# Last feed-forward of a two-block transformer: the down projection set three pairs of tiles behind the gate and up products, in place of two

## What is computed

```
def conv_ffn(h, w_up, taps, conv_b, w_down, rows):
    a, g = jnp.split(h @ w_up, 2, axis=-1)          # width 2816 each
    gc = lax.conv_general_dilated(g2, tp[:, :, None, :].astype(g.dtype), (1, 1), 'SAME', ...)
    gc = gc.reshape(bsz, t, f) + conv_b
    return (a * jax.nn.gelu(gc, approximate=False)) @ w_down

        x = x + g2 * conv_ffn(h2, w_up[l], conv_w[l], conv_b[l], w_down[l], rows)
    return rmsnorm(x, norm_final)
```

## Time and profile before

| what | value |
|---|---|
| median of three executions | 1308.42 us |
| the profiled execution: its time | 1310.74 us |
| its span, first to last instruction | 1308.9 us |
| mean granted TensorE clock | 0.975 |
| TensorE busy over the span | 1220.5 us, 93% |
| VectorE busy | 964.2 us, 74% |
| ScalarE busy | 601.6 us, 46% |
| GpSimd busy | 217.9 us, 17% |

### The profile page before, as it was taken

How to read it: one execution, slowest core, us unless ns; L and a number is a source line. 1 busy time by engine, 2 the same in 40 slices (tenths; PEclk the granted TensorE clock), 3 DMA queues, 4 the chain that set the end, 5 groups by cost and what they waited for, 6 DMA issues and landing times.

```text
span 1308.9 us, 21913 instructions
## 1 busy us (share of the span) xinstructions
PE 1220.5 (93%) x9222; PEld 1133.2 (87%) x9222; DVE 964.2 (74%) x1338; ACT 601.6 (46%) x818; POOL 217.9 (17%) x138
## 2 busy tenths in 40 slices
PE   3999989899999999999899999999899988999997
PEld 3888878677899999996577999999799887999996
DVE  6767665655479886565875699785659946999996
ACT  4464243233554444646365675444442444455442
POOL 0000000000244543000000132222000003344441
PEclk9999899899999999999999999999899998999999
DMA  8351001000577765553322779885352333545540
GB/s 279 132 173 65 2 33 66 1 1 1 193 265 251 255 227 180 169 168 120 105 97 97 255 279 322 287 287 180 110 181 97 101 110 112 181 160 181 188 161 33
DMA packets 122080, 199.74 MB, mean 153 GB/s; under 512 B 3200, under 2 KB 110080, under 8 KB 111744
## 3 DMA queue, kind: packets, MB, share of 16 engines
q1 hardware_dynamic: 117088, 168.11, 38.0%
q0 software_dynamic: 3456, 25.17, 5.4%
q10 hardware_dynamic: 1440, 5.08, 1.1%
HBM read 197.30 MB, written 1.05 MB: 152 GB/s over the span
## 4 chain that ended last, share of the span: by engine, by line
PE 63%; DVE 26%; ACT 6%; issue 4%; DMA 0%; DVEq 0%; ACTq 0%
PE bank L661 11%; PE bank L663 11%; PE bank L662 11%; DVE ring_r L1848 8%; DVE buf L2587 6%; PE bank L748 4%; PE bank L749 4%; PE bank L750 4%; ACT high L1261 4%; DVE work L2139 2%; PE bank L947 2%; DVE work L2135 2%; PE bank L935 2%; PE bank L677 1%; PE bank L1149 1%
## 5 line engine op out<-in xcount | busy, mean ns | idle before, releaser
L661 PE MATMUL bank<-part,high 128*128 128x256 f32 x1664 | 474.1, 285 | 29.0 <-DVE part L1855 22.5
L663 PE MATMUL bank<-part,ring_r 128*128 128x256 f32 x1664 | 468.3, 281 | 0.0
L662 PE MATMUL bank<-part,high 128*128 128x256 f32 x1664 | 468.3, 281 | 0.0
L1848 DVE TENSOR_TENSOR ring_r<-ring,high 128x2048 fp32r<-128x2048 f32 (+1 forms) x155 | 343.3, 2222 | 117.5 <-ACT high L1261 116.7
L1261 ACT ACTIVATE high<-ring 128x2048 fp32r<-128x2048 f32 x155 | 295.6, 1910 | 188.0 <-PE bank L663 135.3
L661 PEld LDWEIGHTS bank<-part,high 128*128 128x128 f32 x1664 | 316.3, 190 | 35.1 <-issue 17.5
L662 PEld LDWEIGHTS bank<-part,high 128*128 128x128 f32 x1664 | 316.1, 190 | 1.3 <-issue 1.2
L663 PEld LDWEIGHTS bank<-part,ring_r 128*128 128x128 f32 x1664 | 316.3, 190 | 0.0
L1776 POOL TENSOR_TENSOR ring_r<-ring,high 128x512 fp32r<-128x512 f32 x44 | 87.9, 2000 | 483.7 <-ACT high L1261 483.7
L748 PE MATMUL bank<-part,high 128*128 128x256 f32 x528 | 150.4, 285 | 5.7 <-DVE ring_r L1848 5.7
L1770 POOL TENSOR_TENSOR part<-buf,part 128x256 fp32r<-128x256 f32 x65 | 116.7, 1797 | 225.9 <-ACT part L1327 225.9
(11 more groups left out here) (276 smaller groups left out, 1555.5 us busy)
## 6 DMA issues: line engine op xcount, KB each, us to landing
ring<-in_wide SPq DMA_DIRECT2D x122, 1024.0 KB, 5.9
ring<-in_down SPq DMA_DIRECT2D x33, 1024.0 KB, 4.9
buf<-in_wide POOLq DMA_DIRECT2D x24, 1024.0 KB, 5.9
con<-in_cons SPq DMA_DIRECT2D x1, 1536.0 KB, 11.1
ring<-in_wide SPq DMA_DIRECT2D x2, 576.0 KB, 7.0
buf<-in_wide ACTq DMA_DIRECT2D x1, 1024.0 KB, 5.2
buf<-in_wide SPq DMA_DIRECT2D x1, 1024.0 KB, 5.3
buf<-in_ctx_t ACTq DMA_DIRECT2D x1, 1024.0 KB, 6.6
```

The lines of the kernel that those rows point to most:

```text
L661: mm(bank, ah, bh, start=start, stop=False, skip_group_check=shared)
L662: mm(bank, ah, bl, start=False, stop=False, skip_group_check=shared)
L663: return mm(bank, al, bh, start=False, stop=stop, skip_group_check=shared)
L1848: v.tensor_tensor(low, raw, hi.bitcast(F32), ALU.subtract).then_inc(sem("unit_low"), 1)
```

## The change

The one constant `LAG = 2` becomes `LAGS = (2, 2, 3)`, indexed by the feed-forward. For the first two the order stays as it was. For the last, the stream, the bank plan, TensorE's order and the `ahead` calls of ScalarE and VectorE all use 3, so TensorE goes g0 g1 g2 g3 d0 g4 d1 ... g10 d7, and d8, d9, d10 are left for the list behind the loop. On VectorE the last turn's `ahead` for a down unit moves from the end of the loop to behind the low part of tile 21; ScalarE's already stood behind `gate_high` of tile 21.

```diff
-LAG = 2
+LAGS = (2, 2, 3)
...
     def ffn(n):
         for c in range(PAIR_N):
             out.extend((f"gu{n}", c, half, "wide", W_AT[f"gu{n}"][0] + c) for half in range(2))
-            if c >= LAG:
-                out.append((f"dn{n}", c - LAG, 0, "down", PAIR_N * n + c - LAG))
-        out.extend((f"dn{n}", c, 0, "down", PAIR_N * n + c) for c in range(PAIR_N - LAG, PAIR_N))
+            if c >= LAGS[n]:
+                out.append((f"dn{n}", c - LAGS[n], 0, "down", PAIR_N * n + c - LAGS[n]))
+        out.extend((f"dn{n}", c, 0, "down", PAIR_N * n + c) for c in range(PAIR_N - LAGS[n], PAIR_N))
...
-                        if c >= LAG:
-                            down_pair(n, c - LAG)
-                    w = [arrived(f"dn{n}", c, 0) for c in range(PAIR_N - LAG, PAIR_N)]
-                    rest = range(FT - 2 * LAG, FT)
+                        if c >= LAGS[n]:
+                            down_pair(n, c - LAGS[n])
+                    w = [arrived(f"dn{n}", c, 0) for c in range(PAIR_N - LAGS[n], PAIR_N)]
+                    rest = range(FT - 2 * LAGS[n], FT)
...
-                    if f % 2 and LAG <= f // 2 < PAIR_N - 1:
-                        ahead("dn2", f // 2 - LAG, 0)
+                    if f % 2 and LAGS[2] <= f // 2 < PAIR_N - 1:
+                        ahead("dn2", f // 2 - LAGS[2], 0)
                 gate_high(2, FT - 2)
                 gelu_of(FT - 1)
                 gate_high(2, FT - 1)
-                ahead("dn2", PAIR_N - 1 - LAG, 0)
+                ahead("dn2", PAIR_N - 1 - LAGS[2], 0)
                 down(2, 7)
...
-                    if f % 2 and f // 2 >= LAG:
-                        ahead("dn2", f // 2 - LAG, 0)
+                    if f % 2 and LAGS[2] <= f // 2 < PAIR_N - 1:
+                        ahead("dn2", f // 2 - LAGS[2], 0)
                 gated(2, FT - 1, slice(0, S))
                 eng.wait_ge(sem("act_high"), 3 * FT)
                 eng.wait_ge(sem("act_ready"), 3 * FT - 1)
                 v.tensor_tensor(act_low(FT - 1), act_value(FT - 1), act_high(FT - 1).bitcast(F32), ALU.subtract).then_inc(sem("act_ready"), 1)
+                ahead("dn2", PAIR_N - 1 - LAGS[2], 0)
                 down_resid(2, lambda cb, bank: v.scalar_tensor_tensor(resid[:, cb, :], bank, ada[:, 40 + cb, 0:1], resid[:, cb, :],
```

More of the change, by code:

```diff
@@ L257, in plan_ffn @@
                     place(key, FFN_BANKS)
-                if c == LAG:
+                if c == LAGS[n]:
                     for j in range(KT // 2):
                         place_at(("dn", n, j), j)
-                if c >= LAG:
-                    unit_mid(f"dn{n}", c - LAG, 0)
+                if c >= LAGS[n]:
+                    unit_mid(f"dn{n}", c - LAGS[n], 0)
             for key in after_first:
                 place(key, FFN_BANKS)
-            for c in range(PAIR_N - LAG, PAIR_N):
+            for c in range(PAIR_N - LAGS[n], PAIR_N):
                 unit_job(f"dn{n}", c, 0, ("dn", n, KT // 2 - 1))
@@ L784, in feed_forward @@
                                 pe.wait_ge(sem("act_ready"), FT * n + f + 1)
-                            last = down_tile(n, f, cb, w[f // 2 - PAIR_N + LAG])
+                            last = down_tile(n, f, cb, w[f // 2 - PAIR_N + LAGS[n]])
                         if cb % 2:
@@ L1345, in ffn @@
                             between(f // 2)
-                            if f // 2 >= LAG:
-                                ahead(f"dn{n}", f // 2 - LAG, 0)
+                            if f // 2 >= LAGS[n]:
+                                ahead(f"dn{n}", f // 2 - LAGS[n], 0)
                 def down(n, norm_no):
@@ L1939, in ffn @@
                         between(f)
-                        if f % 2 and f // 2 >= LAG:
-                            ahead(f"dn{n}", f // 2 - LAG, 0)
+                        if f % 2 and f // 2 >= LAGS[n]:
+                            ahead(f"dn{n}", f // 2 - LAGS[n], 0)
                 for ap, value in ((one_col, 1.0), (eps_lnx, LNX_EPS), (eps_sub, SUBLN_EPS)):
```

## The result

| | before | after |
|---|---|---|
| median of four executions each | 1308.42 us | 1322.87 us |
| the profiled execution: its time | 1310.74 us | 1323.33 us |
| its span | 1308.9 us | 1321.5 us |
| first gate/up matmul to the start of the last down matmul | 199.99 us | 213.37 us |

The change made the kernel slower: the ratio is 1.0088, with a 95% interval from 1.0056 to 1.0121, that is 7.3 to 15.8 us. The forecast was 1322.6. It leaves out what the earlier stages do differently from one execution to the next; in the profiled one after, the stage began 0.8 us earlier.

The account below looks back on a forecast made before the run. TensorE and VectorE were both taken as full, VectorE setting the pace. The last matmul, at 1294.1 + 16.85 + 1.8 = 1312.75 against 1298.54, comes 14.2 us later: 1308.4 + 14.2 = 1322.6 us, range 1317 to 1328.

Parts of the forecast that it names:

- (a): Front of the last feed-forward: TensorE waits for banks 1.7 us before tile 6 and 2.0 before tile 7, at no cost.
- (b): From tile 6 on: VectorE has one down unit fewer behind it and leads by 2.2 us at tile 21's taps.
- (c): Tail: d10's split falls behind tile 21's low part; the list holds d8, d9 and d10, TensorE idle some 14 us.
- (d): Last 144 matmuls to the end: 16.85 us plus 1.8 for the clock's restart (1.6 to 3.5); last matmul 14.2 us later.
- Rival 1: VectorE, middle pairs: it escapes its collisions with GpSimd, so only +5.6 us, 1314.0 us, no change; 4%.
- Rival 2: Tail: the list does not hold d8 and d9, each waits only for itself; +2.7 us, 1311.1 us, no change; 4%.
- Rival 3: Front: the 3.7 us of bank waits reach VectorE and the lead is lost; slower still, 1325 to 1328.5 us; 11%.
- Rival 4: Where TensorE waits for activations: the longer lag helps and the kernel gets faster; the two waits total 5.1 us; 1%.

Follow-up runs that it names:

- e1: The changed kernel with the list of waits ahead of the last down matmuls taken out; ratio 1.0027, stage 201.14 us.
- e3: The changed kernel without the list of waits and with d10 split ahead of tile 21's taps; ratio 1.0000, stage 199.06 us.
- e5: The kernel before (lag 2) with the list of waits taken out; ratio 0.9966, stage 196.78 us.
- e2: The changed kernel, list kept, with rounding and split of d10 moved back ahead of tile 21's taps; ratio 1.0058, stage 206.09 us.
- e4: The changed kernel with the list cut to d9 and d10, so d8 runs straight behind d7; ratio 1.0063, median 1317.86 us.

## Why the prediction was right

**(a) The first pairs.** Expected: 1.7 us before tile 6, 2.0 before tile 7, free of cost in the changed kernel. TensorE waited 1.67 and 1.68 us at 1130.48 (tile 5) and 1138.05 (tile 6), 0.64 at 1144.58 (tile 7). So tile 6 came as expected, while the wait before tile 5 was not foreseen and the one before tile 7 was far shorter than said. VectorE's rows of the taps of tiles 2 and 4 in the kernel after show both misses, and the first two rows here, of TensorE and VectorE in the kernel before, what they stand against (tile 4's taps took 5.66 us there):

```profile
1130.49 0.35 PE L661 MATMUL bank<-part,high 128*128 128x256 f32 x1 [0.63 <-DVE buf L1918]
```
```profile
1125.40 4.61 DVE L2587 SCALAR_TENSOR_TENSOR buf<-buf,col 128x256 f32<-128x256 f32 x8
```
```profile
1124.36 5.65 DVE L2587 SCALAR_TENSOR_TENSOR buf<-buf,col 128x256 f32<-128x256 f32 x8
...
1139.49 4.61 DVE L2587 SCALAR_TENSOR_TENSOR buf<-buf,col 128x256 f32<-128x256 f32 x8
```

Tile 2's taps took 1.0 us more and tile 4's 1.0 less than before, and so in every kernel here with a lag of three; the prediction had kept both as they were. The waits before tiles 5, 6 and 7 came to 4.0 us, where the forecast had 3.7 before tiles 6 and 7 and left out what the kernel before already waits before tile 5, 0.63: that the sums are near each other is luck, since the two misses cancel. In the changed kernel the waits were free, as VectorE reached tile 21 ahead of the kernel before all the same (b), and e1, with all of them, is only 1.2 us behind it in the stage. e3 against e5 shows their price where the tail hides nothing. e3's bank waits are 3.3 us longer (4.69 against 1.35, the 0.72 before tile 4 in both), e5 waits 1.4 us in the tail that e3 doesn't, and the stages lie 2.3 apart; so the front costs about 3.7 us there, restarts of the clock included.

**(b) The middle.** Expected: VectorE 2.2 us ahead by tile 21's taps. From the stage's start they began at 1282.32 - 1097.72 = 184.60, before at 187.38: 2.8 ahead, of which 2.3 is d10's split itself; the other half microsecond is no more than readings of one program differ by.

**(c) The tail.** This was the step that counted. Expected start of the last 144 matmuls 195.55 us into the stage, after 14 us of idle; measured 195.03 after 13.97. e1 and e2 show the two causes apart: without the list the idle is 1.90 us, with the split in its old place it is 5.62, with neither there is none (e3).

**(d) The clock.** Expected 1.8 us for the restart, at most 3.5. The last 143 spacings took 18.34 us where 0.1178 each give 16.85: 1.5 us, a little under my lower bound of 1.6. The windows of the kernel after:

```profile
1278.80:1292.70 13.90, 0.00 (x0) 0.00 (x0) 11.11 (x16) 5.08 (x7) 2.98 (x2) 0.62 0.00 0
1292.70:1296.70 4.00, 3.95 (x21) 3.98 (x22) 0.00 (x0) 0.00 (x0) 0.00 (x0) 0.60 0.00 0
1296.70:1300.70 4.00, 4.00 (x36) 4.00 (x35) 0.00 (x0) 0.00 (x0) 0.00 (x0) 1.00 0.01 4
```

The granted clock (the third number from the end) had fallen during the idle time, was 0.60 in the first 4 us of work and full from there. The sum, 0.5 us too late at the start of the run and 0.3 too much for the clock, gives 14.2 against the 13.4 of the stage. The medians lie 14.45 us apart, the spans 12.6, and the interval of the ratio reaches from 7.3 to 15.8 us, so that forecast and median agree to 0.3 us is luck; what the runs bear out is the hold and its size.

**The rivals.** Rival 1 did not come: VectorE's 176 taps took 107.0 us in all, before 106.8 for the same number, so it lost as much to collisions as ever, though single tiles lost more or less than before (a). Rival 2 was priced at +2.7 us for a kernel in which the list does not hold d8 and d9; e1 is that kernel and came to +1.2 in the stage, the difference being the restart that a wait of 1.90 us did not cost. Rival 3, the front, is right as a mechanism and wrong for this kernel: it costs only where nothing hides it. Its premise that a slow restart follows each wait over 2 us does not hold in the changed kernel, as the last section shows. Rival 4, a gain by later activations, had nothing to gain from.

## What to carry to other kernels

A longer lag helps only against waits for what it delays: look at what ends the idle stretches (here splits of weights and banks, not activations) before lengthening it. Whatever lies behind the loop grows with the lag, so the tail has to be read as a chain of its own: which unit's buffer comes free by what, where in each engine's order its preparation is written, and whether a wait for the last unit stands ahead of work that is ready. Waits written just where they are needed are worth more here than the lag: taking the list out of the kernel before won 3.2 us of the stage by the removal of one line.

## What was not expected of the hardware

The restart of TensorE's clock cost about the same whatever the idle stretch before it. Against 0.1178 us a matmul the runs behind the last hold took 1.5 us more after 13.97 us of idle, 1.8 after 8.67 (e4: 12.95 us for 95 spacings), and 2.0 after 5.62 (e2: 1302.05 - 1283.25 = 18.80 us for 143). After 1.90 us, in e1, it was 0.1. My upper bound, which let the cost grow with the idle time, was not needed.

Whether a wait of some 2 us is followed by a slow restart can't be read from its length. The 6 us behind the wait of 2.05 us in the kernel after, and behind the one of 2.06 us in e3 (the granted clock is the third number from the end):

```profile
1169.78:1175.78 6.00, 6.00 (x53) 6.00 (x53) 5.82 (x7) 0.72 (x1) 3.05 (x2) 1.00 0.47 160
```
```profile
1171.49:1177.49 6.00, 6.00 (x38) 6.00 (x39) 5.82 (x7) 0.72 (x1) 3.03 (x2) 0.72 0.46 155
```

The first kept the full clock, the second was granted 0.72 of it and got 15 matmuls less done. What decides between the two is not shown here.
